# Index keys made by feature instead of by token, and turned in the middle of the query unit

## The reference, cut to what matters

```python
xn = rms_norm(h, norm_mix[l])
proj = xn @ w_in[l]
(q, k, v, qi, ki, wi, sc_u, sc_b, sc_c, rw_z, gate_pre) = jnp.split(proj, split_points, axis=-1)
qi = partial_rope(qi.reshape(bsz, seq, IDX_HEADS, IDX_DIM), positions)
ki = partial_rope(ki.reshape(bsz, seq, 1, IDX_DIM), positions)[:, :, 0]
...
rel = jax.nn.relu(jnp.einsum('bthd,bsd->bths', qi_b, ki).astype(jnp.float32))
isc = jnp.einsum('bths,bth->bts', rel, wi_b.astype(jnp.float32) * idx_scale)
isc = jnp.where(causal[None], isc, -jnp.inf)
_, sel = lax.top_k(isc, k_sel)
```

## Time and profile before

| | us |
|---|---|
| median of 3 runs | 1745.69 |
| lowest, highest | 1745.4, 1747.13 |
| profiled execution | 1742.73 |
| its span | 1740.8 |

### The profile page before, as it was taken

How to read it: one execution, slowest core, us unless ns; L and a number is a source line. 1 busy time by engine, 2 the same in 40 slices (tenths; PEclk the granted TensorE clock), 3 DMA queues, 4 the chain that set the end, 5 groups by cost and what they waited for, 6 DMA issues and landing times.

```text
span 1740.8 us, 30924 instructions
## 1 busy us (share of the span) xinstructions
PE 1699.7 (98%) x13056; PEld 1544.2 (89%) x13056; DVE 1169.7 (67%) x1637; ACT 937.2 (54%) x1378; POOL 186.5 (11%) x208
## 2 busy tenths in 40 slices
PE   7999999999999999999999999999999999999998
PEld 6988999999998988998999998888788988877887
DVE  7867455787877966446787775656766656567664
ACT  5583424554545573335555464665674546657742
POOL 0453400000001645300000000000000100000000
PEclk8999999999999999999999999999999999999998
DMA  6433433455545423523555545434345453343451
GB/s 232 164 127 101 145 133 110 162 179 188 182 159 184 167 101 114 172 98 103 189 198 179 185 168 195 145 122 169 122 149 193 161 203 143 134 157 121 172 191 49
DMA packets 48056, 268.33 MB, mean 154 GB/s; under 512 B 13552, under 2 KB 14448, under 8 KB 16176
## 3 DMA queue, kind: packets, MB, share of 16 engines
q1 hardware_dynamic: 38448, 264.80, 42.6%
q10 hardware_dynamic: 8704, 0.53, 0.3%
q0 software_dynamic: 768, 1.05, 0.2%
HBM read 264.52 MB, written 1.84 MB: 153 GB/s over the span
## 4 chain that ended last, share of the span: by engine, by line
PE 77%; DVE 14%; ACT 5%; issue 1%; POOL 1%; DMA 0%; SPq 0%; POOLq 0%; DVEq 0%; ACTq 0%
PE bank L1358 13%; PE bank L1360 13%; PE bank L1359 13%; PE bank L2453 8%; PE bank L2455 8%; PE bank L2454 8%; DVE w_low L878 5%; ACT arena L2086 2%; ACT arena L615 1%; PE bank L2524 1%; PE bank L1595 1%; PE bank L1596 1%; PE bank L1597 1%; ACT w_high L549 1%; PE bank L2483 1%
## 5 line engine op out<-in xcount | busy, mean ns | idle before, releaser
L878 DVE TENSOR_TENSOR w_low<-slab,w_high 128x2048 fp32r<-128x2048 f32 x250 | 579.9, 2324 | 230.5 <-ACT w_high L549 223.9
L1358 PE MATMUL bank<-act_high,w_high 128*128 128x256 f32 x2304 | 661.6, 287 | 3.9 <-DVE act_low L978 2.9
L1359 PE MATMUL bank<-act_low,w_high 128*128 128x256 f32 x2304 | 653.2, 283 | 0.0
L1360 PE MATMUL bank<-act_high,w_low 128*128 128x256 f32 x2304 | 653.1, 283 | 0.0
L549 ACT ACTIVATE w_high<-slab 128x2048 fp32r<-128x2048 f32 x250 | 473.9, 1896 | 154.9 <-PE bank L2455 80.3
L1358 PEld LDWEIGHTS bank<-act_high,w_high 128*128 128x128 f32 x2304 | 443.2, 192 | 13.4 <-issue 5.7
L1359 PEld LDWEIGHTS bank<-act_low,w_high 128*128 128x128 f32 x2304 | 443.4, 192 | 0.7 <-issue 0.5
L1360 PEld LDWEIGHTS bank<-act_high,w_low 128*128 128x128 f32 x2304 | 443.3, 192 | 0.0
L2453 PE MATMUL bank<-w_high,act_high 128*128 128x512 f32 x768 | 306.0, 399 | 0.7 <-DVE w_low L878 0.7
L2455 PE MATMUL bank<-w_low,act_high 128*128 128x512 f32 x768 | 300.6, 391 | 0.0
L2454 PE MATMUL bank<-w_high,act_low 128*128 128x512 f32 x768 | 300.0, 391 | 0.0
(11 more groups left out here) (239 smaller groups left out, 1731.9 us busy)
## 6 DMA issues: line engine op xcount, KB each, us to landing
slab<-stream_a SPq DMA_DIRECT2D x144, 1024.0 KB, 4.8
slab<-stream_b SPq DMA_DIRECT2D x104, 1024.0 KB, 4.8
residual<-x_t SPq DMA_DIRECT2D x4, 256.0 KB, 5.4
lora_weights<-lora SPq DMA_DIRECT2D x2, 512.0 KB, 8.0
out_t<-residual SPq DMA_DIRECT2D x4, 256.0 KB, 2.2
d_inverse<-arena POOLq DMA_DIRECT2D x2, 256.0 KB, 3.7
constants<-common SPq DMA_DIRECT2D x1, 384.0 KB, 9.6
constants_a<-const_a SPq DMA_DIRECT2D x1, 368.0 KB, 9.8
```

Source lines behind the costliest of these rows:

```text
L878: line.did(line.eng.tensor_tensor(core.wl[u % PARTS][:, 0:SLAB_WIDTH[u]], core.slab[u % SLABS][:, 0:SLAB_WIDTH[u]], core.wh[u % PARTS][:, ...
L1358: eng.matmul(out, wh, xh, start=first, stop=False, skip_group_check=True)
L1359: eng.matmul(out, wh, xl, start=False, stop=False, skip_group_check=True)
L1360: return eng.matmul(out, wl, xh, start=False, stop=last, skip_group_check=True)
```

## The change

The unit `ki` is made by feature: for each of the 8 depths the 40 weight columns are stationary and all 256 tokens move, three products for each, 24 in all. The result has 40 partitions (features) and 256 columns (tokens). ACT copies it to the arena and raises `ki_copied`. A new step `ki_turn` stands between the halves of unit `q 0`: PE waits for `ki_copied` and transposes the two halves of the tokens into the free half of the same bank, and only then counts the product of the unit `ki`; ACT and DVE do there what they did in the unit `ki`. The order of all other steps stays. The table of semaphore counts gains `ki_copied` and `ki_made`.

```diff
@@ schedule_a
     amid(("w", 1), ("sum", 0), ("norm", 0), ("tables", 0))
     put(("w", 1), ("norm_x", 0))
     put(("ki", 0), ("params", 0))
+    amid(("q", 0), ("ki_turn", 0))
     put(("q", 0), ("turns", 0), ("turns", 1))
@@ scalar_a, unit
         elif kind == "ki":
-            made(core, eng, rows, u)
-            for m in range(2):
-                act(index_keys(core)[:, m], bank[banks[0][0]][:, 64 * m:64 * m + IDX_DIM].unsqueeze(1).broadcast_to([P, 4, IDX_DIM]),
-                    ACT.Copy, sem("qk_raw"), scale=token_scale(core, m))
+            eng.wait_ge(*sem("ki_made").next(eng))
+            act(flat(core, REL_)[0:IDX_DIM + IDX_HEADS, :], bank[banks[0][0]][0:IDX_DIM + IDX_HEADS, 0:T], ACT.Copy, sem("ki_copied"))
@@ scalar_a
+    def ki_turn(_):
+        u = UA["ki", 0]
+        b = rows[u][4][0][0]
+        made(core, eng, rows, u)
+        for m in range(2):
+            act(index_keys(core)[:, m], bank[b][:, T + 64 * m:][:, 0:IDX_DIM].unsqueeze(1).broadcast_to([P, 4, IDX_DIM]),
+                ACT.Copy, sem("qk_raw"), scale=token_scale(core, m))
...
@@ vector_a
+    def ki_turn(_):
+        b, spare = rows[UA["ki", 0]][4][0][0], flat(core, AROPE_, 2)
+        eng.wait_ge(*sem("qk_raw").next(eng, 2))
+        for m in range(2):
+            src = bank[b][:, T + 64 * m:][:, 0:IDX_DIM + IDX_HEADS]
+            line.settled()
+            rotate(index_keys(core)[:, m], src[:, 0:IDX_DIM].unsqueeze(1), table(m, 32, 8), table(m, 40, 8), spare[:, T * m:],
+                   None, sem("roped"))
+            did(ts(core.small[:, WI_ + 8 * m:WI_ + 8 * m + 8], src[:, IDX_DIM:], token_scale(core, m),
+                   float(IDX_HEADS ** -0.5 * IDX_DIM ** -0.5), ALU.mult, ALU.mult), sem(f"dve_emptied{b}") if m else None)
@@ tensor_a
+    def ki(u):
+
+        n, b = IDX_DIM + IDX_HEADS, rows[u][4][0][0]
+        eng.wait_ge(sem("slab_split").sem, first + u + 1)
+        wh, wl = (w[(first + u) % PARTS][:, 0:n * KD].rearrange("p (k n) -> p k n", k=KD) for w in (core.wh, core.wl))
+        banks.fill(b, "dve")
+        for k in range(KD):
+            last = gemm(eng, bank[b][0:n, 0:T], (wh[:, k, :], wl[:, k, :]), (core.xh[:, k, :], core.xl[:, k, :]), k == 0, k == KD - 1)
+        last.then_inc(sem("ki_made").sem, 1)
+
+    def ki_turn(_):
+
+        n, b = IDX_DIM + IDX_HEADS, rows[UA["ki", 0]][4][0][0]
+        eng.wait_ge(*sem("ki_copied").next(eng))
+        for m in range(2):
+            ins = eng.transpose(bank[b][:, T + 64 * m:][:, 0:n], flat(core, REL_)[0:n, P * m:P * m + P], core.const("ident")[0:n, 0:n])
+        ins.then_inc(sem("products").sem, 1)
...
```

More of the change, by code:

```diff
@@ L314 @@
     gathered=3, hidden=22, hidden_high=22, hidden_low=22, index_scores=4, index_summed=4, inverses_in=128,
[L315 to L322, removed]
+    inverses_written=16, k_scale=1, keys_ready=1, keys_scaled=1, ki_copied=1, ki_made=1, kk=1, kk_squared=1,
+    kk_summed=1, lora_inputs=1, lora_made=4, lora_out=2, masked=1, maxed=4, mean_square=2, mix_high=4,
+    mix_ready=4, newest_tap=22, norm_spread=2, normed=4, off_diagonal=1, outputs_turned=2, products=84,
+    qk_raw=6, queries_ready=1, reset_made=1, rhs_made=4, rooted=1, rooted_sums=2, roped=6, row_kept=1,
+    sa_made=4, scored=4, silu=22, solved=8, spread_made=4, squared=8, state=3, state_made=3, summed=8,
+    summed_decay=2, tok_made=6, tokens_scaled=1, transposes_in=128, turned=8, u_made=3, weighted=4,
+    x_high=12, x_ready=12, y_made=4, y_mean=2, y_rooted=1, y_scale=1, y_squared=2, y_variance=1, ya_done=2,
+    ya_high=2, yb_high=2, yb_ready=2, yc=2, yc_high=2, yc_ready=2, z_mixed=7,), "b": dict(
     act_emptied0=9, act_emptied1=8, act_emptied2=7, act_emptied5=16, act_emptied6=17, act_emptied7=16,
@@ L843, in scalar_a @@
     walk(SCHEDULE[stage], dict(params=params, root_table=lambda _: act_root_table(core, line), angles=angles, round=act_round(core, line, FIRST_SLAB[stage]), scaled=scaled,
-                               square=square, norm=norm, norm_x=lambda _: high(8), x_ffn=x_ffn, unit=unit, turns=turns, isc=isc,
+                               square=square, norm=norm, norm_x=lambda _: high(8), x_ffn=x_ffn, unit=unit, ki_turn=ki_turn, turns=turns, isc=isc,
                                scores=scores, turn=turn, post=post, lora_inputs=lora_inputs, lora=lora, decay=decay,
@@ L1039, in unit @@
                            spare[:, T * m + 64:], sem(f"dve_emptied{b}"), sem("roped"))
[L1040 to L1049, removed]
         elif kind == "uc":
@@ L1262, in vector_a @@
                                split=dve_split(core, line, FIRST_SLAB[stage]), scaled=scaled, norm=norm, tables=tables,
-                               norm_x=lambda _: normed(8, "norm"), x_ffn=x_ffn, unit=unit, isc=isc, topk=topk, scores=scores, pv=pv, post=post,
+                               norm_x=lambda _: normed(8, "norm"), x_ffn=x_ffn, unit=unit, ki_turn=ki_turn, isc=isc, topk=topk, scores=scores, pv=pv, post=post,
                                decay=decay, kk_root=kk_root, kk_inverse=kk_inverse, kk_scale=kk_scale, keys=keys, mask=mask, solve=solve, scan_y=scan_y, gn=gn, ffn=ffn))
@@ L1559, in begin @@
     def begin(u):
-        if rows[u][0] not in ("q", "w", "ki"):
+        if rows[u][0] not in ("q", "w"):
             begin_(u)
@@ L1569, in unit @@
             return
+        if rows[u][0] == "ki":
+            ki(u)
+            return
         if u not in begun:
@@ L1577, in by_token_half @@
             eng.wait_ge(sem("slab_split").sem, first + u + 1)
[L1578 to L1590, removed]
+        wh, wl = (w[(first + u) % PARTS][:].rearrange("p (k n) -> p k n", k=4) for w in (core.wh, core.wl))
+        b = (fills if i == 0 else rows[u - 1][4])[m][0]
+        if i == 0:
+            banks.fill(b, "dve")
+        out, start, stop = bank[b][:], 0 if i == 0 else -1, 3 if i else -1
+        for k in range(4):
             at = k + 4 * i
@@ L1597, in by_token_half @@
             last = mm(out, high, wl[:, k, :], start=False, stop=k == stop, skip_group_check=True)
-        if m or (i and kind != "ki"):
+        if m or i:
             last.then_inc(sem("products").sem, 1)
@@ L1871, in gn @@
                 ins.then_inc(sem("g_made").sem, 1)
-    walk(SCHEDULE[stage], dict(begin=begin, unit=unit, sum=sums, spread=spread_row, norm_x=norm_x, turns=turns,
+    walk(SCHEDULE[stage], dict(begin=begin, unit=unit, sum=sums, spread=spread_row, norm_x=norm_x, ki_turn=ki_turn, turns=turns,
                                isc=isc, scores=scores, turn=turn, pv=pv, post=post, lora=lora, kk_sum=kk_sum, kk_spread=kk_spread, keys=keys,
```

## The result

| | before | changed kernel |
|---|---|---|
| median of 20 runs each, us | 1743.56 | 1746.25 |
| lowest, highest | 1740.39, 1747.13 | 1743.89, 1751.05 |
| profiled execution's span | 1740.8 | 1745.5 |

The ratio is 1.0017, with a 95% interval of 1.0009 to 1.0025: 3.0 us slower, 1.6 to 4.4, a ratio under the 0.2% that I had set as the bound, with an interval that reaches beyond it. (With 20 runs instead of 3 the median of before is 1743.56, not 1745.69. The two medians are 2.7 us apart.) The forecast was 1.76 us slower, and its range of 1743.5 to 1751.0 holds the measured 1746.25.

What follows compares the result with a forecast made beforehand. PE, busy 1699.7 of 1740.8 us, was taken as the bound, with ACT and DVE arriving about when it finishes `ki`. Shifts of -0.74 and +2.50 us in the two layers summed to +1.76, 1747.4 us; range 1743.5 to 1751.0.

Steps and rivals of the forecast that it cites:

- What is removed and added: PE in `ki` and `q 0`: durations alone cut its work by 7.2 us in layer one, 3.96 in layer two.
- The first wait: Amid `q 0`, PE's transposes wait for ACT's copy of `ki`: 3.4 us in layer one, 3.35 in layer two.
- The second wait: At `turns 0`, PE waits for DVE's rotation behind `split 5`; `q 1` begins 0.74 us earlier, in layer two 2.50 later.
- That both shifts reach the end: Behind `q 1`: PE releases what follows, so -0.74 and +2.50 us both reach the end, +1.76 us.
- The low clock in `q 0` is hidden: Second half of `q 0`: low clock follows the 3.4 us wait, 5.2 us instead of 2.8, without delaying the turns.
- The clock behind the second wait: Rival, `q 1` in both layers: low clock costs 2 x 1.57 = 3.1 us, giving 1750.5; chance 0.18.
- Only the first wait holds: Rival, at `turns 0`: rotation comes in time, `q 1` follows `q 0` directly; 1741.3 to 1746.1 us; chance 0.12.
- the whole gain comes: Rival, `ki` and `q 0`: no wait is born, -11.2 us, 1734.5; chance 0.04.
- The 40 stationary columns cost as much as before: Rival, new `ki` products: PE reaches its wait for the copy up to 3 us later; forecast stays; no separate chance.
- Low clock elsewhere: Rival, outside these stretches: stretches of low clock, such as at 129.57 us, fall differently; no size given; chance 0.04.

Runs made afterwards that it cites:

- experiment 1: Changed kernel with PE's 24 products of unit `ki` made twice; median 1746.48 us, ratio 1.0026 against the kernel before.
- experiment 4: Kernel before, 48 products kept, with only ACT's copies and DVE's rotation of the index keys moved behind `round 5` and `split 5`; 1746.41 us, ratio 1.0026.
- experiment 2: Changed kernel with unit `ki` ahead of `round 4` and `split 4`, so ACT copies earlier; 1750.74 us, ratio 1.0047 against the kernel before.
- experiment 5: Changed kernel with ACT's copy ahead of `round 4` and DVE's rotation ahead of `split 5`; 1744.72 us, ratio 1.0008 against the kernel before.
- Experiment 3: Changed kernel with `round 5` and `split 5` behind unit `q 0`, so DVE rotates right behind `split 4`; 1743.96 us, ratio 0.9998 against the kernel before.
- experiment 6: Changed kernel with transposes behind all of `q 0`, `round 5` and `split 5` behind the rotation, turns amid `q 1`; 1740.1 us, ratio 0.9984 against before.
- experiment 7: Kernel before, 48 products kept, with `turns 0` and `turns 1` between the halves of `q 1`; 1741.03 us, ratio 0.9993.

## Why the prediction was right, point by point

The time moved the way that was forecast, by 3.0 us (1.6 to 4.4) where 1.76 was forecast, and the trace of the stretches says 1.99: -0.70 in the first layer and +2.69 in the second, where -0.74 and +2.50 were forecast. It is these two numbers that bear the mechanism out; the runs alone could not, since their interval is wider than the forecast is large. The absolute figures stood on a median of before that was 2.1 us too high: on 1743.56 the same sum gives 1745.3, not 1747.4. In the following the first layer's starts are less 0.81 and the second's less 1.67, by which the norm's spread began later in the profile of after.

- **What is removed and added.** 24 products at 0.12 us: 3.0 us, forecast 2.88. The first one has 0.31 us to the next, a pause behind the norm's spread; the first narrow one had 0.21 where the next had 0.12. Two transposes 0.25, forecast 0.2. The copy 0.36, forecast 0.38.
- **The first wait.** The copy began at 36.31 (forecast 36.30) and PE went on at 36.72 (36.76). The wait was 3.05 us, not 3.4: PE arrived 0.1 later, and its records end with the last product's tail.
- **The second wait.** `round 5` began at 37.16 (37.2), `split 5` at 39.17 (39.13), the rotation ended at 42.81 (42.77), the turns began at 42.86 (42.85) and `q 1` at 43.71 (43.64). In the second layer the turns began at 555.60 (555.48) and `q 1` at 556.45 (556.27). The handover from the transposes to `round 5` took 0.54 there, since the transposes met the low clock, and I had 0.43; the turns took 0.85, and I had 0.79. These are the 0.2 us by which the sum was short.
- **That both shifts reach the end.** The turns' wait is answered by DVE, DVE by ACT, ACT by PE's transposes; behind `q 1` everything is released by PE. No later wait took the shifts up: the time between the stretches and the time behind them were not shorter than before (491.66 and 490.10, 1181.77 and 1181.34 us). Shown by the trace alone; the differences that the clock makes are as large as the effect.
- **The low clock in `q 0` is hidden.** Right: it fell (0.71 and 0.74) and the turns began no later. In experiment 1 the same half ran at the high clock and the turns began 15.36 us behind the spread all the same. In the second profile of the changed kernel the low clock held the second layer's `q 0` longer, PE's wait shrank to 0.41, and the turns began at 15.48, where the first profile had 15.47.
- **The clock behind the second wait.** Forecast as a rival of 0.18, it did not come in either profile of the changed kernel (a wait of 1.49 and 1.44 us, in the second profile 1.28 and 0.41), not behind 2.88 us in experiment 1, and not behind 1.83 and 1.80 in experiment 4. It came behind 4.39 us in experiment 2 and behind 2.26 in experiment 5, at 1.5 to 2.2 us a layer (I had 1.57 from the second layer of before). The length of the wait alone doesn't decide it. What it does to the unprofiled runs wasn't seen.
  The Trainium skill's rule of the page "TensorE: Matmul & The Clock Gate", section "Part 4: PE-mode transpose", that transposes don't count as work for the clock, could not be tested apart: in the kernel before and in experiments 3, 6 and 7 the eight transposes stood between full work, in the others directly behind a wait (in experiment 4 in the second layer alone). Taken alone it would have brought a low `q 1` in the changed kernel in both layers, and it came in neither of two profiles.
- **Only the first wait holds; the whole gain comes.** Both wrong in the changed kernel. Experiment 3 made the first of the two by taking away the second wait: 1743.96 us where the prediction had 1741.3 to 1746.1.
- **The 40 stationary columns cost as much as before.** They didn't (3.01 us). That the wait would have taken up 3 us more, as the prediction said, is shown by experiment 1.
- **Low clock elsewhere.** I gave it 0.04 and no price. It did fall otherwise, 10.2 us instead of 6.8 between the layers' stretches, which is 1.56 of the 4.79 us in the spans, nearly as much as the change's own 1.99. That term was missing in the sum. The right direction doesn't hang on it, but the nearness of the run's +3.0 to a forecast without it is in part luck.

What stays open: by their stretches alone, experiments 1, 4 and 6 lie outside the intervals of their runs, and experiment 2 at the edge. With the time between the stretches all but experiment 4 lie inside, experiment 5 at the edge. For experiment 4 (+2.1 in the profiles, 3.0 to 6.3 in the runs) a low clock behind the wait in part of the executions would do it, but neither of its two profiles shows one. And why a kernel has one, two, three or four of the 3.4 us at the low clock between its layers was not tested.

## What to carry to other kernels

That an engine is busy 98% doesn't say that less work on it is less time. Before shortening its work, note when the others reach the steps that it will wait for, by their order of instructions: the gain ends there. Here ACT and DVE were due at the same moment as PE, so 7 us less work on PE gave 0.7 us in one layer, and 4 us less cost 2.7 in the other, since the rotation that PE's turns wait for now stood behind the rounding and splitting of one more slab. The change gained (6 us in the stretches, 0.3 to 5.2 in the runs) only when PE had the rest of `q 0` to do while ACT made the copy, and the rotation stood ahead of a split that wasn't urgent.

## What the runs showed of the hardware that I had not expected

- Moving 256 columns over 40 stationary ones kept the granted clock at 1.00 through the unit (3.01 us), where 40 columns moving over 128 stationary ones had brought it to a mean of 0.67 in the first layer (in the second the unit ran at 1.00, and the clock fell behind it, to a mean of 0.76 in `q 0`).
- A shorter first wait made a kernel slower: in experiment 2 the wait for the copy fell by 1.8 us, the wait before the turns grew to 4.39, and the clock, now high in `q 0`, was low in the turns (1.62 us instead of 0.85) and `q 1` (7.03 instead of 5.62).
- The same work of 490 us took 488.55 to 493.41 us by the number of its stretches at the low clock, 1.6 us for each 3.4. The stretches of before repeated within 0.05 us in three profiles, where twenty runs gave the difference of the whole time to 1.4. But a stretch tells only of itself: the time between the two added 1.6 us in both profiles of the changed kernel.
